# Differential attention in a tuned two-model kernel: the 16 first queries of all heads taken at once, one-pass masks, later and smaller first loads

## What is computed

```python
def diff_attention(q, k, v, lam_p, subln_g, lambda_init, valid, pos):
    lam = jnp.exp(jnp.sum(lp[0] * lp[1])) - jnp.exp(jnp.sum(lp[2] * lp[3])) + lambda_init
    q = rope(q...) * DA_DH ** -0.5          # 8 heads, 2 maps of 64 each
    k = rope(k...)
    s = jnp.einsum('bqhmd,bkhmd->bhmqk', qb, k)
    allowed = (key_pos[None, :] <= q_pos[:, None]) & valid[None, :]
    p = jax.nn.softmax(jnp.where(allowed, s, MASK_VALUE), axis=-1)
    w = p[:, :, 0] - lam * p[:, :, 1]
    o = jnp.einsum('bhqk,bkhe->bqhe', w, v)
    o = _rms(o) * subln_g * (1.0 - lambda_init)
```

## Time and profile before

| | |
|---|---|
| runs, median (lowest, highest) | 2629.0 us (2626.05, 2629.96) |
| profiled execution, its own time | 2622.89 us |
| its span, first to last instruction | 2621.1 us |
| busy: PE, weight loads | 96%, 91% |
| busy: DVE, ACT, POOL | 54%, 52%, 76% |
| mean granted TensorE clock | 0.985 |
| DMA | 354.9 MB, 135 GB/s over the span |

### The profile page before, as it was taken

One profiled execution on the slowest core, in us unless ns is written; L12 is line 12 of the kernel. 1 busy time (PEld: TensorE's weight loads), 2 busy tenths in 40 slices (PEclk: granted clock), 3 DMA queues, 4 the chain that ended last, 5 costly groups with the idle time before them and its releaser, 6 DMA issues.

```text
span 2621.1 us, 49419 instructions
## 1 busy us (share of the span) xinstructions
PE 2503.8 (96%) x19316; PEld 2375.3 (91%) x19316; DVE 1417.5 (54%) x2624; ACT 1359.3 (52%) x2372; POOL 1980.3 (76%) x2171
## 2 busy tenths in 40 slices
PE   8999999999999999999999999979889998998999
PEld 7999999999999889899999987768789998788999
DVE  7775433458727865343558554644445446855550
ACT  5534555556645334556456555552364456665543
POOL 8956668899889856669899986350169998666997
PEclk9999999999999999999999999899999999999999
DMA  7533344456565423345457654120036665333665
GB/s 213 146 97 105 113 117 142 124 166 183 167 181 146 133 85 105 113 121 153 138 171 214 197 154 121 51 79 1 20 110 194 186 176 145 97 106 107 194 189 155
DMA packets 683222, 354.92 MB, mean 135 GB/s; under 512 B 11152, under 2 KB 681072, under 8 KB 682608
## 3 DMA queue, kind: packets, MB, share of 16 engines
q1 hardware_dynamic: 680464, 343.45, 45.8%
q10 hardware_dynamic: 2528, 8.31, 0.9%
HBM read 350.67 MB, written 1.05 MB: 134 GB/s over the span
## 4 chain that ended last, share of the span: by engine, by line
PE 71%; POOL 12%; DVE 9%; ACT 4%; issue 2%; DMA 2%; ACTq 0%; DVEq 0%
PE pb L277 70%; POOL wl L346 12%; ACT pool L300 1%; ACT wh L335 1%; DVE bx L3385 1%; DMA raw<-in_w_in 1%; DVE pool L1123 1%; PE pb L554 1%; DMA raw<-in_ffn_w 0%; DMA raw<-in_w_ffn_in 0%; DVE pool L1109 0%; ACT bx L300 0%; DVE pool L1137 0%; DVE pool L3424 0%; DVE pool L3562 0%
## 5 line engine op out<-in xcount | busy, mean ns | idle before, releaser
L346 POOL TENSOR_TENSOR wl<-raw,wh 128x256 fp32r<-128x256 f32 (+1 forms) x2164 | 1972.9, 948 | 630.5 <-ACT wh L335 630.1
L277 PE MATMUL pb<-xh,wh 128*128 128x272 f32 (+2 forms) x3104 | 943.7, 304 | 21.7 <-POOL wl L346 4.7
L335 ACT ACTIVATE wh<-raw 128x1024 fp32r<-128x1024 f32 (+2 forms) x669 | 690.5, 1033 | 454.0 <-PE pb L277 269.4
L277 PE MATMUL pb<-xl,wh 128*128 128x272 f32 (+2 forms) x3104 | 891.3, 287 | 0.0
L277 PE MATMUL pb<-xh,wl 128*128 128x272 f32 (+2 forms) x3104 | 890.9, 287 | 0.0
L277 PEld LDWEIGHTS pb<-xh,wh 128*128 128x128 f32 x3104 | 593.2, 191 | 48.7 <-issue 18.3
L277 PEld LDWEIGHTS pb<-xl,wh 128*128 128x128 f32 x3104 | 593.4, 191 | 3.9
L277 PEld LDWEIGHTS pb<-xh,wl 128*128 128x128 f32 x3104 | 592.5, 191 | 0.0
L277 PE MATMUL pb<-pool 128*128 128x128 f32 (+14 forms) x2048 | 305.1, 296 | 41.7 <-DVE pool L1137 7.3
L277 PEld LDWEIGHTS pb<-pool 128*128 128x128 f32 (+5 forms) x2048 | 235.4, 174 | 87.9 <-issue 20.9
L277 PE MATMUL pb<-u2h,wh 128*128 128x256 f32 x840 | 239.8, 285 | 4.1 <-DVE u2l L648 4.1
(11 more groups left out here) (398 smaller groups left out, 3770.2 us busy)
## 6 DMA issues: line engine op xcount, KB each, us to landing
raw<-in_w_in SPq DMA_DIRECT2D x208, 512.0 KB, 3.7
raw<-in_ffn_w SPq DMA_DIRECT2D x120, 512.0 KB, 3.9
raw<-in_w_ffn_in SPq DMA_DIRECT2D x88, 512.0 KB, 3.9
raw<-in_w_branch SPq DMA_DIRECT2D x48, 512.0 KB, 3.9
raw<-in_od_w_in SPq DMA_DIRECT2D x41, 512.0 KB, 3.8
raw<-in_w_ffn_out SPq DMA_DIRECT2D x32, 512.0 KB, 4.6
raw<-in_ev_w_in SPq DMA_DIRECT2D x20, 512.0 KB, 3.9
raw<-in_w_out SPq DMA_DIRECT2D x16, 512.0 KB, 3.9
```

The costliest lines, as they stand in the source:

```text
L277: return e.matmul(out, lhsT=l, rhs=r, start=a, stop=z, skip_group_check=True)
L335: E.e.activation(hi, src, ACT.Copy).then_inc(*sig("weight_hi", ("hi", g)))
L346: E.e.tensor_tensor(lo[:, s, :], src[:, s, :], hi[:, s, :].bitcast(F32), SUB).then_inc(*sig("weight_lo", *[("lo", g, i) for i in ks]))
```

## The change

It has three parts.

1. The third query tile goes. The 16 first queries of all 8 heads are put side by side into one 128x128 operand (`SHORT_Q`), scored against the 16 first keys of the heads with one matmul per map, masked by a predicated copy that keeps each head's own causal 16x16 block (mask 17), and go once per layer through maximum, exponential, scaling and one transpose. ACT copies each head's 16x16 block out with the head's second unit. A layer then has 16 units. All blocks of the other two tiles are turned by full 128x128 transposes. The rate falls from 0.82 to 0.6.
2. The identity and `neg` are rounded to float32r in place (`IDONE`, `NEGONE`), and the masks of differential and latent attention are float32r matmuls. The differential attention's masks always cover 128 columns.
3. The masks come as uint8 straight into `msk` with no cast. The rotation angles (`c1` to `s2`, 128x1088) and decays (`dm` and `inv3`, 128x1089) are loaded later, in steps 1 and 4 of `a_hgrn_prep`, and dq and `ret` wait for them.

```diff
-    ident, ones = C("ident"), C("ones")
+    ident, ones, neg = IDONE[:, :].bitcast(F32), C("ones"), NEGONE[:, :].bitcast(F32)
...
     def v_scalars(E):
...
         e.wait_ge(*at("in2"))
-        e.tensor_copy(msk[:, :, :], POOL[:, 12288:12288 + MASKS * P].rearrange("p (a b) -> p a b", b=P)).then_inc(
-            *sig("sc_v", ("msk",)))
...
-        c0 = cplan["p1"][0]
-        e.dma_start(cst[:, c0:], A["consts"][:, c0:]).then_inc(*landed("in2"))
-        yield
-        e.dma_start(POOL[:, 12288:12288 + MASKS * P], A["masks"]).then_inc(*landed("in2", ("in2",)))
+        c0, c1 = cplan["p1"][0], cplan["c1"][0]
+        e.dma_start(cst[:, c0:c1], A["consts"][:, c0:c1]).then_inc(*landed("in2"))
+        yield
+        e.dma_start(msk[:, :, :], A["masks"].rearrange("p (a b) -> p a b", b=P)).then_inc(*landed("in2", ("in2",)))
...
+        e.wait_ge(*at("in2"))
+        e.activation(IDONE[:, :], C("ident"), ACT.Copy)
+        e.activation(NEGONE[:, :], C("neg"), ACT.Copy).then_inc(*sig("sc_a", ("one_pass",)))
...
         for u in range(14):
             hp, part = divmod(u, 3)
+            if li == 0 and u in (1, 4):
+                late_consts(e, u == 4)
...
+    def v_short_max(e, a):
+        e.wait_ge(*at("sh_scores", a.name))
+        for m_ in range(2):
+            e.copy_predicated(SHORT[:, m_, :], msk[:, 17, :], banks[7 - m_][:, 0:P]).then_inc(*sig("at_v"))
+        e.tensor_reduce(SHORT_S, SHORT.rearrange("p m (h k) -> p m k h", k=NM), X, MAX)
+        e.tensor_reduce(SHORT_ST[:, 0:2], SHORT_S, X, MAX, negate=True)
...
     def pe_att(E, a):
+        e.wait_ge(*at("sh_q", a.name))
+        for m_ in range(2):
+            r = slice(64 * m_, 64 * m_ + 64)
+            m = mm(e, banks[7 - m_][:, 0:P], SHORT_Q[r, :], DK[r, :, 0:NM], True, True)
+        m.then_inc(*sig("at_scores", ("sh_scores", a.name)))
         e.wait_ge(*at("at_zero", a.name))
...
-                    mm(e, B[0:nq, nk - nq:nk], ident[:, 0:nq], C("neg")[:, 0:nq], False, True).then_inc(
+                    mm(e, B[:, nk - P:nk], IDONE[:, :], NEGONE[:, :], False, True).then_inc(
...
-                    if qn == P:
-                        t = e.transpose(B[0:kn, off:off + qn], pb[:, 0, k0:k0 + kn], ident)
-                    else:
-                        t = mm(e, B[0:kn, off:off + qn], pb[:, 0, k0:k0 + kn], ident[:, ql - q0:ql - q0 + qn], True, True)
+                    t = e.transpose(B[:, off:off + P], PB[:, (u - 1) % 2, k0:k0 + P], ident)
+                if u == 1:
+                    e.wait_ge(*at("sh_prob", a.name))
+                    e.transpose(banks[7][:, 288:288 + P], SHORT[:, 0, :], ident)
...
     def a_att(E, a):
+        e.activation(SHORT_Q.rearrange("p (h k) -> p h k", k=NM), DQ[:, :, 0:NM], ACT.Copy)
         a_pad(E, a, 0)
+        e.wait_ge(*at("sh_max", a.name))
+        for m_ in range(2):
+            act(E, SHORT_S[:, m_, :], SHORT_S[:, m_, :], ACT.Exp, bias=SHORT_ST[:, m_:m_ + 1],
+                acc=SHORT_ST[:, 2 + m_:3 + m_]).then_inc(*sig("at_exp", ("sh_exp", a.name, m_)))
...
+                    o = 288 + NM * hh
+                    e.wait_ge(*at("sh_turn", a.name))
+                    t = e.activation(wt[0][0:NM, 0:NM], banks[7][0:NM, o:o + NM], ACT.Copy)
...
-                [(144, 128, 272), (16, 128, 144), (0, 16, 16)], KT3, PBV, turned_weights(), (3, 4, 5, 6, 7), 32,
+                [(144, 128, 272), (16, 128, 144)], KT3, PBV, turned_weights(), (3, 4, 5, 6, 7), 32,
...
     def v_diff(E, li):
+        e.memset(SHORT, -1e30).then_inc(*sig("at_v"))
+        e.wait_ge(*last("at_v"))
+        e.memset(PB[:, 1, NM + P:2 * P], 0.0).then_inc(*sig("at_v"))
...
-        mm(e, B[:, P:NS + P], ident, C("neg").unsqueeze(1).broadcast_to([P, 2, P]), False, True).then_inc(
+        mm(e, B[:, P:NS + P], IDONE[:, :], NEGONE[:, :].unsqueeze(1).broadcast_to([P, 2, P]), False, True).then_inc(
...
-            w_in("hg", "copy", bg, 0.82, dst=HGR)
+            w_in("hg", "copy", bg, 0.6, dst=HGR)
```

More of the change, by code:

```diff
@@ L218, in program @@
     cplan, ncst = const_plan()
+    n0 = cplan["neg"][0]
+    with nc.sbuf_tensor("idone", [P, P], F32R) as IDONE, nc.sbuf_tensor("toneg", [P, n0 - P], F32), \
+            nc.sbuf_tensor("negone", [P, P], F32R) as NEGONE:
+        pass
     cst = sb("cst", [P, ncst])
@@ L549, in pe_turn @@
         r = E.banks(1)[0]
+        if p.name == "hi0" and j == 0:
+            E.e.wait_ge(*at("one_pass"))
         E.e.wait_ge(*at("staged", p.name, j))
@@ L587, in v_rope_tile @@
         e.wait_ge(*at("mm", g))
+        if p.name == "dq0" and j == 0:
+            e.wait_ge(*at("in_angles"))
         if j >= 2:
@@ L1385, in v_att @@
                 pb, st = a.probs[u % 2], a.stats(u)
+                if u == 0:
+                    v_short_max(e, a)
                 yield
@@ L1438, in a_att @@
             e.wait_ge(*at(*q))
+        e.activation(SHORT_Q.rearrange("p (h k) -> p h k", k=NM), DQ[:, :, 0:NM], ACT.Copy).then_inc(
+            *sig("at_exp", ("sh_q", a.name)))
         a_pad(E, a, 0)
+        e.wait_ge(*at("sh_max", a.name))
+        for m_ in range(2):
+            act(E, SHORT_S[:, m_, :], SHORT_S[:, m_, :], ACT.Exp, bias=SHORT_ST[:, m_:m_ + 1],
+                acc=SHORT_ST[:, 2 + m_:3 + m_]).then_inc(*sig("at_exp", ("sh_exp", a.name, m_)))
         for u in range(len(a.units) + 1):
@@ L1452, in a_att @@
                 yield
-                if qi == 1 and hh + 1 < a.heads:
+                if qi == 0 and hh + 1 < a.heads:
                     a_pad(E, a, hh + 1)
@@ L3923, in constants @@
     put("inv3", inv3)
-    m = np.zeros((P, MASKS, P), np.float32)
+    m = np.zeros((P, MASKS, P), np.uint8)
     a, b = i[:, None], i[None, :]
```

49 lines of the change are left out of this document (41 added, 8 removed).

## The result

The changed kernel took 2603.7 us (median of 10 runs, 2594.7 to 2626.3). The kernel before, run again beside it, took 2629.4 us (median of 10, 2618.1 to 2635.6). The ratio is 0.9905, with a 95% interval of 0.9879 to 0.9931: faster by 25.7 us, where 31.3 were forecast. In microseconds the interval reaches from 18 to 32, so the medians alone don't tell the two apart. The profiled execution took 2600.8 us (span 2599.0 us), 22.1 us less than that of before.

What follows compares the result with a forecast made beforehand. PE was taken as the bound, carrying 71% of the chain and filling the differential attention. Terms 7.8 + 12.5 + 8.3 - 3.0 + 2.0 + 1.2 + 2.5 = 31.3 us lowered the median from 2629.0 to 2598 us; range 2589 to 2613.

Steps and rivals of the forecast that it cites:

- The slower rate: Differential attention: background rate 0.6 for 0.82 shrinks the value matmuls' waits for turned blocks; 2 us back, bounds 0 and 3.1.
- The third unit's scores: Differential attention, PE: 0.49 us of scores gone for each of 16 heads, 7.8 us.
- Turning: Differential attention, PE: full transposes for two units, none for the third; 0.78 us per head, 12.5 us.
- Masks: Differential attention, PE: 64 float32r masks at 0.08 us in place of 0.21, 8.3 us gained.
- The first rival: One-pass masks keep their price, 0.19 us each with the weight load not hidden: 2605 us; chance 0.08.
- The starts: Start of each layer's attention: added memsets, unit 1's delay in layer 0 and short transposes give back 3.0 us.
- Unit 1's wait: Layer 0's attention start: unit 1's second score comes about 1.9 us later than PE could take it.
- The short transpose: Each layer's attention: the one added transpose for the short queries costs 0.1 us per layer.
- The second rival: Value matmuls wait more for ACT's copies behind exponentials, pad and weight copy; 8 to 16 us lost, about 2610; chance 0.12.
- Latent attention: Latent attention, PE: 8 masks of 256 columns go from 0.42 to 0.12 us; half counted, 1.2 us (0 to 2.4).
- First loads: Kernel start, near 37 us: smaller early loads remove POOL's 2.48 us wait; 2.5 us gained, bounds 0 and 4.1.
- The test for the stretch from first scores to last scaling: Sign of being right: this attention stretch shorter by 12 to 14 us in each layer, with equal weight matmuls.

Runs made afterwards that it cites:

- pool_stands: Changed kernel with QZ's memsets first, first maxima earlier, ACT's pad behind copies and square, credit remainder 0.2, and POOL waiting for one DVE subtraction: 2590.7 us, ratio 0.9872.
- f32_masks: Changed kernel with the masks of both attentions multiplied as float32 again, 128 columns wide: 2600.1 us.
- narrow_turns: Changed kernel with blocks of 16 queries turned by 16-column identity matmuls again: 3.2 us lost in either layer; whole time not given.
- rate_082: Changed kernel with the attention's background rate at 0.82 again in place of 0.6: 2595.0 us.
- pad_behind: Changed kernel with ACT's pad of queries moved behind the copies of the turned blocks: each layer won 1.0 us; whole time not given.
- first_max: Changed kernel with the first unit's maxima and exponentials one step earlier: layer 0 won 12.5 us in place of 10.7; whole time not given.
- changed_again: The changed kernel run once more, unaltered, for a second profile: 2606.1 us.
- remainder: Changed kernel with the background credit's remainder set to 0.2 behind layer 0's attention: ratio 0.9884 to the kernel before.
- first_loads: Kernel before with only the later first loads (byte masks without cast, constants in three pieces): 2624.9 us.

## Why the prediction was right, and where it was off

The direction, the place and the size were right: 2603.7 us lies in 2589 to 2613. The sum was 5.6 us too high. The large terms were right. The slower rate brought less than its 2.0 us, and the sum had nothing for what the rate does behind layer 0's attention. Step by step:

- **The third unit's scores, 7.8.** No 16-column scores are left. No run undid this part alone; its size rests on the rows of before.
- **Turning, 12.5.** By the rows 0.23 + 0.23 + 0.34 per head, 12.8; by the run 6.4 of the first two's 7.4.
- **Masks, 8.3.** Measured 7.1 to 7.4: a mask costs 0.095 us (0.21 less 0.115), not 0.08. The first rival (0.19 each, no gain) fell in the run with float32 masks. With it falls, for these short streams too, the rule of the Trainium skill, TensorE: Matmul & The Clock Gate, section The mechanism, that a weight load overlaps matmuls in flight only when the row group differs: the masks' load rows are 190 ns long here (median), and the mask with its own load adds half of that. The same section also lets a load into the background weight buffer go ahead of matmuls in flight, and that agrees with the trace.
- **The starts, 3.0.** The first scores' group grew from 3.05 to 3.19 us in layer 0 although its masks are 0.23 cheaper, so 0.37 for the 0.45. Unit 1's wait cost 1.8 with its restarts for the 1.9, at the place named (the run with the earlier maximum took it away). Its reason was only half seen: that the addition stands ahead of the first maximum is itself the slower rate's doing, since at 0.82 it stands behind. The short transpose costs 0.11. In layer 1, with the clock up in both kernels, it is 0.33 and 0.11. About 2.7 us together.
- **The slower rate, 2.0 back.** This term was too high. PE's idle times for turned blocks were 1.1 and 3.1 us before and 2.2 and 2.3 after, under "issue", so by them nothing came back. By the measure of the prices the value matmuls' groups took 1.1 us less (0.6 more in layer 0, 1.7 less in layer 1, clock up in both), and those of the square's sum took 0.4 more: 0.7 for the 2.0. The longer distance was counted, but not the further weight copies that ACT gets into it; that these are the reason isn't shown. The second rival named the right chain (copies behind exponentials, pad and weight copy), and the pad in it was worth 1.0 us a layer, but the waits did not grow by its 8 to 16 us.
- **Not in the sum: 3.6 us lost behind layer 0's attention** (2.1 for the wait, 1.5 for the clock). I compared the orders inside the attention and took the number 0.6 to end at its edge. Its remainder reached beyond it.
- **Latent attention, 1.2.** Below what the granted clock changes there from run to run.
- **First loads, 2.5.** Measured 3.0. The gap of POOL shrank by 1.5 us only; what is late next is ACT's wait for the lambda sums.

7.8 + 12.8 + 7.4 - 2.7 + 0.7 = 26.0 us for the attentions, where the two stretches show 25.7; with 3.0 and less 3.6, 25.4 against the 25.7 of the medians. That these two agree so well is luck, as the interval is 7 us wide on either side. The profiled pair shows 22.1, with the 4.7 us lost from the end of layer 1's attention on. One further part of that is visible. In the changed kernel one subtraction of DVE took 6.59 us, the pair 6.92, and PE waited behind it; DVE and PE in order of time:

```profile
1540.51 6.92 DVE L2118 TENSOR_TENSOR pool<-pool,rs 128x256 f32<-128x256 f32 x2 [6.20 <-ACT rs L304]
...
1552.32 2.93 PE L281 MATMUL pb<-bx,cst 128*128 128x256 f32 x6 [7.03 <-ACT bx L2432]
```

In the kernel before the pair took 1.95 and PE waited 4.70 us there. It is one more of the hold-ups: POOL's run ends at 1546.81 us, the subtraction 0.28 us later. The rest of the 4.7 us I can't assign piece by piece; granted clocks differ there in every profile.

The test for the stretch from first scores to last scaling was badly chosen. At the slower rate the attention spreads over more weight matmuls, so that stretch stayed at 139 us in layer 0 (270.57 to 409.5 before, 266.50 to 405.9 after) while 10.7 us were won. Equal work has to be enclosed by rows outside the part whose rate changes.

## What to carry to other kernels

In a stretch that PE fills, small float32 products on PE are worth removing, and their price can be read to a few hundredths of a microsecond from the starts of the neighbouring matmuls. A rate or credit that interleaves streams has a phase; after changing it, compare the orders of all engines beyond the part it governs. Place a copy that PE waits for ahead of everything on its engine that nobody waits for yet. And where POOL runs without a pause, look for DVE instructions far longer than the shortest of their kind.

## What the runs showed of the hardware that I had not expected

- A DVE instruction with both inputs in SBUF can be kept out by a run of POOL's. The same subtraction of 1088 columns reached DVE in thirteen profiles (all but that of pool_stands) during the same POOL instruction, its 1120th split. In nine it took 1.3 to 1.5 us, and the next split 1.8 in place of 0.75. In four it took 9.6, past twelve further splits, until POOL's run had ended. Its partner alone took 1.28. 35 shorter instructions of DVE were kept out in the same way (experiments, POOL stands still), at one place in all fourteen profiles. The Trainium skill, SBUF — State Buffer, section Who interferes with whom, says that a DVE instruction with two SBUF inputs contends with a GpSimd instruction that reads SBUF, and that the lock on the shared ports is exclusive. The nine agree, while in the four DVE was not served when the running instruction ended.
- Behind PE's wait of 1.7 us at the start of layer 1's attention the granted clock fell from 2.4 to 1.2 GHz in six profiles of kernels with that wait (the changed one, f32_masks, narrow_turns, rate_082, pad_behind, first_max), and in two more with it (changed_again, remainder) not at all. With the 2.2 us of before it fell once (before) and once not (first_loads), and with 1.1 us in none of four. The fall cost 1.6 us. Behind the wait of 1.8 us that follows layer 0's attention it fell in two profiles and stayed up in four.
- A float32 product with 16 columns of the identity costs more than a full transpose of 128: a narrow one and a transpose 0.46 us, two transposes 0.22.
